# A decoder-style block on one core: the embedding projection moved ahead of its gate, the sums into X moved inside the gate tiles

## The chip, the cores and the metric

The kernel runs on 1 NeuronCore of one Trainium2 chip. The metric is device time in microseconds (us) of one launch; three runs of the kernel before gave 3404.55, 3404.18 and 3402.21, median 3404.18. PE is TensorE, DVE VectorE, ACT ScalarE, POOL GpSimd, and SP issues most of the DMAs.

## The reference

Two blocks run one after the other on a sequence of 512 tokens of width 1024, batch 1, all in float32. The first has two layers (feed-forward, attention and convolution mixer, feed-forward, and a gated per-layer embedding) and ends in a norm; the second has four layers with other mixers. The change touches only the last step of each layer of the first block:

```python
def first_block(x, p, ...):
    h = x
    for i in range(DEPTH):                       # DEPTH = 2
        h = h + 0.5 * swiglu(rmsnorm(h, g_ff1[i]), w_ff1_in[i], w_ff1_out[i])
        h = h + hybrid_mixer(rmsnorm(h, g_mix[i]), ...)
        h = h + 0.5 * swiglu(rmsnorm(h, g_ff2[i]), w_ff2_in[i], w_ff2_out[i])
        gate = sigmoid(rmsnorm(h, g_ple[i]) @ w_ple_gate[i])    # 1024 x 1024
        h = h + gate * (p[i] @ w_ple_proj[i])                   # 256 x 1024
    return rmsnorm(h, g_final)
```

The projection `p[i] @ w_ple_proj[i]` does not depend on `h`.

## The kernel before, in words

**Layout.** `X` holds h turned, as 8 chunks of 128 channels x 512 tokens. A matrix product is a `Gemm`: a list of tiles, one for each 128 output channels, each made of units of up to 8 chunks of 128 input channels. To reach float32 exactness each operand is split into a rounded high half and a low half: the activations into `UH` and `UL` (for the feed-forward's inner vector `HH` and `HL`, for the turned embedding `PH` and `PL`), the weights, loaded into `RAW` by SP, into `WH` (ACT, `high`, line 292) and `WL` (POOL, line 270). Each chunk then takes three matmuls: high x high (line 345), high weights x low activations (346), low weights x high activations (334). A unit of 8 chunks is 24 matmuls, a projection tile (2 chunks) 6. Two PSUM banks take the tiles in turn.

**Order.** Nothing is scheduled: each engine runs a list written by hand, `Step` after `Step`, and waits on semaphores in that order. Within a `Gemm`, PE runs tile n and then `tensor_tail(n)`; ACT runs `high` for a later unit, then the tile's activation (`t.act`), then `scalar_tail(n)`; DVE empties the bank of tile n and runs the tile's `vec`. In a `Gemm` with a root, ACT splits the weights of unit n + 2 between the end of tile n on PE and the activation of tile n. `high` waits for the unit two before its own.

**The norm.** The gain is in UH and UL; the factor 1/rms is applied behind the matmul, when DVE multiplies a bank by `R` (line 385, into `PRE`). A root makes R: PE sums squares over the partitions with a matmul by ones (line 490, or line 520 for one chunk of squares, 942 where the sum goes to columns), ACT takes the square root (line 495), DVE the reciprocal (line 501).

**The stage around the change**, `ple(l)`, once a layer, behind the feed-forward's output Gemm: `Gate` has 8 tiles of 8 chunks; ACT writes the sigmoid of tile c to `G[:, c, :]` (line 2200). Behind its tile 4 stand the turns of the embedding (`Flips`, 8 transposes, line 2147) and their split (lines 2152, 2155). Then `Proj`, 8 tiles of 2 chunks: DVE multiplies the bank by G (line 2210, into bank `SCALED`), adds to X (2215), and makes the next stage's low half one chunk late (`st.low`, line 911); ACT makes the high half and the square of chunk n - 1 in `scalar_tail(n)` (`st.halves`, lines 901 and 904); PE sums that square behind projection tile n (`total.tensor_chunk(n - 1)`, line 520 or 942). `Close` does chunk 7. In layer 0 the next stage is a feed-forward Gemm that reads UH and UL; in layer 1 it is the final norm, so there are no halves, and ACT also issues six loads for a later stage behind gate tile 1.

Of the kernel before, what the change touches and what calls it, by code (L numbers as in the profile page):

```python
# [117 lines left out]
def chunks(ap):  # L118
    return ap.rearrange("(c p) n -> p c n", p=P)
# [1310 lines left out]
def build(nc, out, a):  # L1430
    with ExitStack() as ctx:
# [93 lines left out]
        with ExitStack() as ph:  # L1525
            sb("GATES", [P, 2 * DC, SEQ], F32, ph)
            with ExitStack() as sub:
                sb("GAP_PLE", [P, 32], F32, sub)
                PH, PL = sb("PH", [P, 2, SEQ], F32R, sub), sb("PL", [P, 2, SEQ], F32R, sub)
                PST = sb("PST", [P, TT, PLE], F32, sub)  # L1530
# [241 lines left out]
        def ffn(l, w_in, w_out, next_gain, beside, kind=Gemm):  # L1772
# [364 lines left out]
        def ple(l):  # L2137

            nonlocal u_ready
            v = m.vec  # L2140
            wg, wp = chunks(a["w_ple_gate"][l]), chunks(a["w_ple_proj"][l])
# [19 lines left out]
            class LoadP(Step):  # L2161
                need = m.splits.total

                def issue(self, e):
                    e.wait_ge(m.splits.sem, self.need)
                    e.dma_start(PST[:], a["p"][l, 0].rearrange("(t p) f -> p t f", p=P)).then_inc(ple_in, 16)
            load_p = LoadP()
            add(load_p)
            last = l == 1
            turn_at = 4  # L2170
            u_all = m.splits.total
            fl = Flips(m, [flip_p(c) for c in range(2)], splits=2)
            fl.t0 = 0

            class Gate(Gemm):
# [8 lines left out]

                def sync_tail(self, e, i, j):
                    if j == turn_at + 1:
                        load_p.issue(e)

                def tensor_tail(self, e, i, n):
                    if n == turn_at:  # L2190
                        fl.tensor(e)

                def vector_tail(self, e, i, n):
# [3 lines left out]
                    if n == turn_at:  # L2197
                        fl.vector(e)
            add(Gate(m, 1, [Tile([(lambda i, c=c: wg[:, :, c * P:(c + 1) * P], DC, 0)], U,
                                 act=lambda e, i, pre, fun, c=c: e.activation(G[:, c, :], pre, ACT.Sigmoid))  # L2200
                            for c in range(DC)], rhs_ready=u_ready, root=Root(m, D)))
            gates = m.act_out.total
            st = Chunked(m, None if last else (lambda c: gcol("g_ff1", c + DC)))
            total = (LateColumnRoot if last else LateRoot)(m, st)

            def proj(c):
                def f(g, e, i, ps):
                    e.wait_ge(m.act_out.sem, gates)
                    e.wait_ge(*v.last)
                    e.tensor_tensor(m.SCALED, ps, G[:, c, :], ALU.mult).then_inc(*g.frees())  # L2210
                    if c > 0:
                        st.low(e, c - 1)
                    e.wait_ge(m.acc_free[g.bank(c)], g.free(0, c) + 1)
                    x = m.X[:, c, :]
                    e.tensor_tensor(x, x, m.SCALED, ALU.add).then_inc(*v.gives(m.x_new.sem, st.x0 + c + 1))
                return f

            class Proj(Gemm):


                def scalar_tail(self, e, i, n):
                    if n == 0:
                        e.activation(B.ES[:, 0:1], m.EPSC[:], ACT.Sqrt)
                    if n > 0:
                        st.halves(e, n - 1)
# [1341 lines left out]
```

## Time and profile before

| | us |
|---|---|
| median of three runs | 3404.18 |
| span of the profiled execution, first to last instruction | 3401.4 |
| PE busy | 3301.1 (97%) |
| DVE busy | 1848.6 (54%) |
| POOL busy | 1385.9 (41%) |
| ACT busy | 1113.3 (33%) |

The profiled execution has no time of its own beside its span; the median of the runs lies 2.8 us above that span. "Busy" counts the time in which an engine's instructions run, not what they wait for. PE's granted clock is near full over nearly the whole span. The stage `ple(0)` lies at about 1098 to 1168 us, `ple(1)` at about 2248 to 2317 us.

### The profile page before, as it was taken

To read this page: it belongs to the slowest core of one execution; us is meant where nothing else is said; L and a number is where in the kernel's file an instruction comes from. 1 tells how busy PE (TensorE), PEld (TensorE's weight loads), DVE (VectorE), ACT (ScalarE), POOL (GpSimd) and SP (SyncE) were. 2 spreads that over 40 slices of the span, in tenths; PEclk is the share of its full clock that TensorE was granted. 3 is DMA by queue.
4 is the path that set the end of the run, shared out by engine and by line. 5 is a ranking of instruction groups with operands and counts; after the bars stand their busy time and mean duration, and the time that the engine had idled before them with its cause. 6 is when DMAs were issued, how large, how long until landed. Compare 5 with 4: busy or idle time off the path is not lost.

```text
span 3401.4 us, 44063 instructions
## 1 busy us (share of the span) xinstructions
PE 3301.1 (97%) x16322; PEld 2611.0 (77%) x16322; DVE 1848.6 (54%) x2928; ACT 1113.3 (33%) x1836; POOL 1385.9 (41%) x691
## 2 busy tenths in 40 slices
PE   9999999999999999999999999999999999999998
PEld 7888877778888788887777888887776666777676
DVE  5532378875433464234888643335545648575753
ACT  4222234422222422223443222223234642344332
POOL 4444454444444344444544444443242223322342
PEclk9999999999999999999999999999999989999999
DMA  5333332244433334333313443344642222322221
GB/s 147 93 116 92 106 88 66 60 122 135 131 89 110 102 120 146 88 102 95 81 44 101 127 133 91 94 155 124 212 131 60 59 57 68 60 46 69 84 86 50
DMA packets 632956, 335.01 MB, mean 98 GB/s; under 512 B 97774, under 2 KB 622703, under 8 KB 631247
## 3 DMA queue, kind: packets, MB, share of 16 engines
q1 hardware_dynamic: 608062, 286.80, 30.4%
q10 hardware_dynamic: 23680, 44.32, 3.6%
q8 instruction: 110, 1.80, 0.2%
q0 software_dynamic: 1040, 1.57, 0.1%
q14 instruction: 64, 0.52, 0.0%
HBM read 308.65 MB, written 23.98 MB: 98 GB/s over the span
## 4 chain that ended last, share of the span: by engine, by line
PE 83%; DVE 11%; issue 3%; ACT 2%; POOL 0%; DVEq 0%; DMA 0%; ACTq 0%; POOLq 0%
PE ps L345 25%; PE ps L334 25%; PE ps L346 24%; PE ps L1138 2%; PE ps L1172 1%; PE ps L1162 1%; DVE UH L440 1%; PE ps L520 1%; DVE TURN L449 1%; DVE UL L443 1%; DVE ps L864 1%; DVE UL L855 0%; DVE SS L452 0%; DVE PRE L385 0%; PE ps L1289 0%
## 5 line engine op out<-in xcount | busy, mean ns | idle before, releaser
L270 POOL TENSOR_TENSOR WL<-RAW,WH 128x1024 fp32r<-128x1024 f32 (+4 forms) x606 | 1297.3, 2142 | 1977.3 <-ACT WH L292 1976.7
L345 PE MATMUL ps<-UH,WH 128*128 128x512 f32 x3056 | 1218.5, 399 | 48.1 <-DVE UL L855 16.4
L346 PE MATMUL ps<-UL,WH 128*128 128x512 f32 x3056 | 1195.8, 391 | 0.0
L292 ACT ACTIVATE WH<-RAW 128x1024 fp32r<-128x1024 f32 (+4 forms) x605 | 571.0, 945 | 1170.6 <-PE ps L334 1126.7
L334 PE MATMUL ps<-UH,WL 128*128 128x512 f32 x3056 | 802.7, 394 | 0.7 <-POOL WL L270 0.7
L345 PEld LDWEIGHTS ps<-UH,WH 128*128 128x128 f32 x3056 | 574.5, 188 | 206.5 <-issue 43.9
L334 PEld LDWEIGHTS ps<-UH,WL 128*128 128x128 f32 x3056 | 570.0, 187 | 132.9 <-issue 12.5
L346 PEld LDWEIGHTS ps<-UL,WH 128*128 128x128 f32 x3056 | 574.8, 188 | 121.4 <-issue 4.5
L345 PE MATMUL ps<-HH,WH 128*128 128x512 f32 x704 | 273.9, 389 | 0.0
L346 PE MATMUL ps<-HL,WH 128*128 128x512 f32 x704 | 273.9, 389 | 0.0
L385 DVE TENSOR_TENSOR PRE<-ps,R 128x512 f32<-128x512 f32 x144 | 99.4, 691 | 293.1 <-PE ps L334 289.4
L1782 DVE TENSOR_TENSOR ps<-ps,R 128x512 f32<-128x512 f32 x88 | 61.6, 700 | 326.7 <-PE ps L334 325.9
L458 DVE SCALAR_TENSOR_TENSOR X<-ps,X 128x512 f32 x48 | 33.1, 689 | 321.8 <-PE ps L334 321.8
L1791 ACT ACTIVATE FUN<-PRE 128x512 f32<-128x512 f32 x88 | 55.6, 632 | 425.9 <-DVE PRE L385 425.9
L334 PE MATMUL ps<-HH,WL 128*128 128x512 f32 x704 | 180.4, 389 | 0.0
L346 PEld LDWEIGHTS ps<-HL,WH 128*128 128x128 f32 x704 | 132.2, 188 | 27.4
L345 PEld LDWEIGHTS ps<-HH,WH 128*128 128x128 f32 x704 | 132.2, 188 | 27.4
L334 PEld LDWEIGHTS ps<-HH,WL 128*128 128x128 f32 x704 | 132.2, 188 | 27.4
L1879 DVE SCALAR_TENSOR_TENSOR ps<-CA,PV,ps 128x512 f32<-128x512 f32 x168 | 127.0, 756 | 6.1
L1229 ACT ACTIVATE S<-ps,NM 128x128 f32<-128x128 f32 (+3 forms) x128 | 66.3, 524 | 91.1 <-DVE NM L1186 76.8
L440 DVE TENSOR_SCALAR UH<-X,PV x48 | 91.0, 1896 | 7.7 <-DVE X L458 7.7
L1199 DVE TENSOR_SCALAR S<-S,RINV 128x128 f32<-128x128 f32 (+3 forms) x128 | 81.5, 678 | 0.0
(447 smaller groups left out, 3441.1 us busy)
## 6 DMA issues: line engine op xcount, KB each, us to landing
RAW<-w_ff_in SPq DMA_DIRECT2D x176, 512.0 KB, 3.8
RAW<-w_in SPq DMA_DIRECT2D x72, 512.0 KB, 3.9
RAW<-w_ff_out SPq DMA_DIRECT2D x64, 384.0 KB, 3.4
RAW<-w_ff_out SPq DMA_DIRECT2D x64, 320.0 KB, 3.1
RAW<-d_w_in SPq DMA_DIRECT2D x24, 512.0 KB, 3.8
CM<-cm_dram ACTq DMA_DIRECT2D x8, 1088.0 KB, 10.5
RAW<-b_w_in SPq DMA_DIRECT2D x17, 512.0 KB, 3.7
RAW<-w_out SPq DMA_DIRECT2D x16, 512.0 KB, 3.8
```

The source lines that it names most:

```text
L270: e.tensor_tensor(m.WL[:, s, 0:k, :], m.RAW[:, r, 0:k, :], m.WH[:, s, 0:k, :].bitcast(F32), ALU.subtract).then_inc(m.low_ready.sem, 1)
L292: e.activation(m.WH[:, s, 0:k, :], m.RAW[:, r, 0:k, :], ACT.Copy).then_inc(m.high_ready.sem, 1)
L334: return e.matmul(out, m.WL[:, s, c, 0:t.cols], H[:, k0 + c, :], start=False, stop=last)
L345: e.matmul(out, m.WH[:, s, c, 0:t.cols], H[:, k0 + c, :], start=(x == 0 and c == 0), stop=False)
L346: e.matmul(out, m.WH[:, s, c, 0:t.cols], L[:, k0 + c, :], start=False, stop=False)
L385: ins = t.pre(e, i, pre, ps) if t.pre else e.tensor_tensor(pre, ps, m.R[0:t.cols, :], ALU.mult)
L440: e.tensor_scalar(high, src, gain, None, ALU.mult).then_inc(*v.next())
L1138: e.matmul(out(x, n), self.q(h, n), self.k(h, n), start=True, stop=False)
L1199: e.tensor_scalar(B.S[:, r, 0:kk], B.S[:, r, 0:kk], B.RI[:, r:r + 1], None, ALU.mult).then_inc(*v.gives(m.normed.sem, self.b + a + 1))
L1229: e.activation(B.S[:, c, 0:kk], m.ps[:, 2 + x % 2, 0:kk], ACT.Exp, bias=B.NM[:, c:c + 1], accum_out=B.RS[:, c:c + 1]).then_inc(m.exped.sem, 1)
L1782: e.tensor_tensor(m.WORK, ps, m.R[:], ALU.mult).then_inc(*g.frees())
L1879: e.scalar_tensor_tensor(dst, src, wj, y, ALU.mult, ALU.add).then_inc(*v.next())
```

## The change

The embedding is loaded behind the fourth weight load of the second feed-forward, and turned and split between that feed-forward's two Gemms. `Proj` now stands before `Gate`, and ACT copies its banks to G. The product with the sigmoid and the sum into X are the `vec` of each gate tile. The square of chunk n - 1 and its sum on PE are in the tails of gate tile n. The high halves, which overwrite what the gate tiles read, are made in `Close`, behind the last gate tile. `SQ` and `ROOT` are the two halves of the buffer shown as TURN.

```diff
@@ ffn
+            g1.embed = embed
             add(g1)
...
             add(Gemm(m, (FC - HELD) // 2, pair_of_tiles(HELD // 2), vec_per_iter=4, rhs_ready=u_ready, splits=2))
+            if embed is not None:
+                embed_turns[embed] = turn_embedding(embed)
+                add(embed_turns[embed])
@@ ple (turn_embedding holds flip_p and its Flips, unchanged)
+            class Proj(Gemm):
+                def scalar_tail(self, e, i, n):
+                    b = self.bank(n)
+                    e.wait_ge(m.unit_done.sem, self.unit(i, n + 1) + 1)
+                    e.activation(G[:, n, :], m.ps[:, b, :], ACT.Copy).then_inc(m.acc_free[b], 1)
+
+                def vector(self, e):
+                    m.wait_tiles(e, self.t0 + self.nt)
+            add(Proj(m, 1, [Tile([(lambda i, c=c: wp[:, :, c * P:(c + 1) * P], 2, 0)], (PH, PL)) for c in range(DC)],
+                     rhs_ready=embed_turns[l].s0))
+
+            class Summed(Chunked):
+                def squared(self, c):
+                    return (m.SQ[:], m.T2[:], m.T[:], m.ROOT[:])[c % 4]
+
+                def square(self, e, c):
+                    e.wait_ge(m.x_new.sem, self.x0 + c + 1)
+                    if c >= 4:
+                        e.wait_ge(m.square_used.sem, self.u0 + c - 3)
+                    e.activation(self.squared(c), m.X[:, c, :], ACT.Square).then_inc(m.x_squared.sem, 1)
+
+                def high(self, e, c):
+                    e.wait_ge(m.x_new.sem, self.x0 + c + 1)
+                    e.activation(m.UH[:, c, :], m.X[:, c, :], ACT.Copy, scale=self.gain(c)).then_inc(m.x_high.sem, 1)
+
+            def gate(c):
+                def f(g, e, i, ps):
+                    e.tensor_tensor(m.SCALED, g.fun, G[:, c, :], ALU.mult).then_inc(*v.next())
+                    if last or c < DC - 1:
+                        self_add(e, c)
+                return f
+
+            def self_add(e, c):
+                x = m.X[:, c, :]
+                e.wait_ge(*v.last)
+                e.tensor_tensor(x, x, m.SCALED, ALU.add).then_inc(*v.gives(m.x_new.sem, st.x0 + c + 1))
 
             class Gate(Gemm):
                 def scalar_tail(self, e, i, n):
                     if last and n == 1:
                         e.wait_ge(m.splits.sem, u_all)
                         for k in range(SETS):
                             load_lr(e, k)
                             load_cm(e, k)
-                def sync_tail(self, e, i, j):
-                    if j == turn_at + 1:
-                        load_p.issue(e)
+                    if n > 0:
+                        st.square(e, n - 1)
 
                 def tensor_tail(self, e, i, n):
-                    if n == turn_at:
-                        fl.tensor(e)
+                    if n > 0:
+                        total.tensor_chunk(e, n - 1)
...
             class Close(Step):
                 def scalar(self, e):
-                    st.halves(e, DC - 1)
+                    e.activation(B.ES[:, 0:1], m.EPSC[:], ACT.Sqrt)
+                    if not last:
+                        e.wait_ge(m.unit_done.sem, done + 1)
+                        for c in range(2):
+                            st.high(e, c)
+                        st.square(e, DC - 1)
+                        for c in range(2, DC):
+                            st.high(e, c)
+                    else:
+                        st.square(e, DC - 1)
 
                 def vector(self, e):
-                    e.wait_ge(*v.last)
-                    st.low(e, DC - 1)
+                    if not last:
+                        st.low(e, 0)
+                        v.last = v.sem, v.n
+                        self_add(e, DC - 1)
+                        for c in range(1, DC):
+                            st.low(e, c)
                     e.wait_ge(*v.last)
@@ Opening
+            def sync_tail(self, e, i, j):
+                if self.embed is not None and j == 3:
+                    load_embedding(e, self.embed, self.u_all)
```

How the instructions stand now, first on ACT in the middle of the gate tiles of layer 0. Before, each gate tile's sigmoid (line 2200) is followed by the weight split of a later unit and the next sigmoid:

```order
L2200 ACTIVATE G<-PRE 128x512 [waits acc_free1]
L292 ACTIVATE WH<-RAW 128x1024 [waits unit_done,raw_ready2]
L2200 ACTIVATE G<-PRE 128x512 [waits acc_free0]
L292 ACTIVATE WH<-RAW 128x1024 [waits unit_done,raw_ready3]
L2200 ACTIVATE G<-PRE 128x512 [waits acc_free1]
```

In the changed kernel the sigmoid is line 2243, and the square of the chunk before is line 2203:

```order
L292 ACTIVATE WH<-RAW 128x1024 [waits unit_done,raw_ready1]
L2243 ACTIVATE FUN<-PRE 128x512 [waits acc_free1]
L2203 ACTIVATE T<-X 128x512 [waits x_new]
L292 ACTIVATE WH<-RAW 128x1024 [waits unit_done,raw_ready2]
L2243 ACTIVATE FUN<-PRE 128x512 [waits acc_free0]
L2203 ACTIVATE T<-X 128x512 [waits x_new]
L292 ACTIVATE WH<-RAW 128x1024 [waits unit_done,raw_ready3]
```

Each sigmoid is now followed by the square of the chunk before it; the weight split still stands ahead of the sigmoid.

Second, PE at the end of a gate tile of layer 0. Before, the eight low-weight matmuls of one tile are followed by the first matmul of the next:

```order
L345 MATMUL ps<-UH,WH 128x512 [waits splits]
L346 MATMUL ps<-UL,WH 128x512
L334 MATMUL ps<-UH,WL 128x512 [waits low_ready]
L334 MATMUL ps<-UH,WL 128x512 x7
L345 MATMUL ps<-UH,WH 128x512 [waits splits,high_ready,acc_free0]
L346 MATMUL ps<-UL,WH 128x512
```

In the changed kernel the sum of a square (line 520, which waits for `x_squared`) stands between them:

```order
L345 MATMUL ps<-UH,WH 128x512 [waits splits]
L346 MATMUL ps<-UL,WH 128x512
L334 MATMUL ps<-UH,WL 128x512 [waits low_ready]
L334 MATMUL ps<-UH,WL 128x512 x7
L520 MATMUL ps<-T,ONES 128x512 [waits x_squared]
L345 MATMUL ps<-UH,WH 128x512 [waits splits,high_ready,acc_free0]
L346 MATMUL ps<-UL,WH 128x512
```

The sum came here from behind the projection tiles; the next gate tile's matmuls stand behind it.

Third, ACT at the end of the gate tiles of layer 0, in the changed kernel (2254 loads the square root's table, 2207 makes a high half):

```order
L2243 ACTIVATE FUN<-PRE 128x512 [waits acc_free0]
L2203 ACTIVATE T<-X 128x512 [waits square_used,x_new]
L2254 ACT_TABLE_LOAD
L2254 ACTIVATE ESINK<-EPSC 128x1
L2207 ACTIVATE UH<-X,PV 128x512 [waits x_new,unit_done]
L2207 ACTIVATE UH<-X,PV 128x512 [waits x_new]
L2203 ACTIVATE TURN<-X 128x512 [waits square_used,x_new]
L2207 ACTIVATE UH<-X,PV 128x512 [waits x_new] x6
L292 ACTIVATE WH<-RAW 128x1024 [waits unit_done,raw_ready2]
```

Before, the high half and the square of each chunk alternate, one pair behind each projection tile. Now all eight high halves stand behind the last gate tile and the table load.

## Rows read from the trace of the kernel before

**Rows 1.** The page's chain that ended last, by engine.

```profile
PE 83%; DVE 11%; issue 3%; ACT 2%; POOL 0%; DVEq 0%; DMA 0%; ACTq 0%; POOLq 0%
```

**Rows 2.** Busy time by stretch: us, then PE, PEld, DVE, ACT, POOL, clock, DMA, GB/s.

```profile
1098.04:1180.53 82.49, 76.28 (x316) 57.58 (x314) 38.87 (x45) 34.38 (x50) 30.30 (x19) 1.00 0.29 83
2248.14:2316.57 68.43, 65.58 (x315) 52.93 (x313) 28.45 (x37) 25.44 (x38) 25.46 (x17) 1.00 0.51 171
```

**Rows 3.** Timeline of PE, first gate tiles, layer 0: start, us, engine, line, what, [idle].

```profile
1098.04 0.39 PE L345 MATMUL ps<-UH,WH 128*128 128x512 f32 x1
...
1104.01 1.13 PE L490 MATMUL ps<-SS,ONES 128*128 128x512 f32 x2 [0.37 <-DVE SS L452]
...
1105.20 0.39 PE L346 MATMUL ps<-UL,WH 128*128 128x512 f32 x1
...
1116.31 0.39 PE L345 MATMUL ps<-UH,WH 128*128 128x512 f32 x1
...
1121.75 0.39 PE L345 MATMUL ps<-UH,WH 128*128 128x512 f32 x1
```

**Rows 4.** Timeline of PE, first projection tiles of layer 0.

```profile
1144.44 0.39 PE L345 MATMUL ps<-PH,WH 128*128 128x512 f32 x1
...
1149.30 1.12 PE L520 MATMUL ps<-TURN,ONES 128*128 128x512 f32 x2 [1.28 <-ACT TURN L904]
...
1150.49 0.39 PE L346 MATMUL ps<-PL,WH 128*128 128x512 f32 x1
```

**Rows 5.** Timeline of ACT, a gate tile and the first projection tiles, layer 0.

```profile
1116.57 1.06 ACT L292 ACTIVATE WH<-RAW 128x1024 fp32r<-128x1024 f32 x1 [3.76 <-PE ps L334]
1117.54 0.61 ACT L2200 ACTIVATE G<-PRE 128x512 f32<-128x512 f32 x1
...
1146.32 1.28 ACT L2223 ACT_TABLE_LOAD   x1
1147.61 0.20 ACT L2223 ACTIVATE ESINK<-EPSC 128x1 f32<-128x1 f32 x1
...
1148.03 0.71 ACT L901 ACTIVATE UH<-X,PV 128x512 fp32r<-128x512 f32 x1
1148.64 0.61 ACT L904 ACTIVATE TURN<-X 128x512 f32<-128x512 f32 x1
```

**Rows 6.** Timeline of DVE, layer 0.

```profile
1109.98 1.35 DVE L385 TENSOR_TENSOR PRE<-ps,R 128x512 f32<-128x512 f32 x2
...
1146.22 0.70 DVE L2210 TENSOR_TENSOR ps<-ps,G 128x512 f32<-128x512 f32 x1 [0.89 <-ACT G L2200]
1146.95 0.69 DVE L2215 TENSOR_TENSOR X<-X,ps 128x512 f32<-128x512 f32 x1
...
1148.84 0.75 DVE L911 SCALAR_TENSOR_TENSOR UL<-X,PV,UH 128x512 fp32r<-128x512 f32 x1
```

**Rows 7.** Timeline of ACT and its DMA issues, layer 1.

```profile
2261.57 0.34 ACTq L2343 DMA_DIRECT2D LR<-lr_dram  x1
...
2264.30 0.42 ACTq L2348 DMA_DIRECT2D CM<-cm_dram  x1
...
2316.57 0.26 ACT L957 ACTIVATE RSUM<-ps,EPSC 128x4 f32<-128x4 f32 x1 [1.33 <-PE ps L942]
```

**Rows 8.** Waits of PE (timeline) and clock of 12 us around them (windows, PE alone).

```profile
10.14 0.47 PE L345 MATMUL ps<-UH,WH 128*128 128x512 f32 x1 [2.12 <-DVE UL L911]
...
5.00:17.00 12.00, 7.89 (x36) 1.00 1.00 296
...
2884.68 0.50 PE L345 MATMUL ps<-UH,WH 128*128 128x512 f32 x1 [2.15 <-ACT WH L292]
...
2880.00:2892.00 12.00, 9.85 (x37) 0.86 0.28 69
...
2469.05 0.47 PE L345 MATMUL ps<-UH,WH 128*128 128x512 f32 x1 [3.40 <-issue]
...
2465.00:2477.00 12.00, 8.60 (x31) 0.86 0.61 172
```

More of the change, by code:

```diff
@@ L1525, in build @@
         with ExitStack() as ph:
[L1526 to L1530, printed above, removed]
+            sb("GAP_PLE", [P, 32], F32, ph)
+            sb("HALVES_USED", [P, 2 * FC, SEQ], F32, ph)
+            PH, PL = sb("PH", [P, 2, SEQ], F32R, ph), sb("PL", [P, 2, SEQ], F32R, ph)
+            sb("TABLES_USED", [P, 832], F32, ph)
+            PST = sb("PST", [P, TT, PLE], F32, ph)
         with ExitStack() as ph:
@@ L2135, in mixer, with load_embedding, turn_embedding @@
             u_ready = g2.s0
-        def ple(l):
-            nonlocal u_ready
+        embed_turns = {}
+        def load_embedding(e, l, ready):
+            e.wait_ge(m.splits.sem, ready)
+            e.dma_start(PST[:], a["p"][l, 0].rearrange("(t p) f -> p t f", p=P)).then_inc(ple_in, 16)
+        def turn_embedding(l):
             v = m.vec
-            wg, wp = chunks(a["w_ple_gate"][l]), chunks(a["w_ple_proj"][l])
             def flip_p(c):
@@ L2173, in ple @@
             fl.t0 = 0
+            return fl
+        def ple(l):
+            nonlocal u_ready
+            v = m.vec
+            wg, wp = chunks(a["w_ple_gate"][l]), chunks(a["w_ple_proj"][l])
+            last = l == 1
+            class Proj(Gemm):
[18 more added lines that the diff above has]
+                    e.activation(m.UH[:, c, :], m.X[:, c, :], ACT.Copy, scale=self.gain(c)).then_inc(m.x_high.sem, 1)
+            u_all = m.splits.total
+            def gate(c):
[8 more added lines that the diff above has]
+                e.tensor_tensor(x, x, m.SCALED, ALU.add).then_inc(*v.gives(m.x_new.sem, st.x0 + c + 1))
@@ L2196, in vector_tail @@
                         e.memset(DEC[:, :, :, 0:1], 0.0).then_inc(*v.next())
[L2197 to L2203, printed above, removed]
@@ L2218, in ple @@
[L2218 to L2225, printed above, removed]
-                def tensor_tail(self, e, i, n):
-                    if n > 0:
-                        total.tensor_chunk(e, n - 1)
+            gates = Gate(m, 1, [Tile([(lambda i, c=c: wg[:, :, c * P:(c + 1) * P], DC, 0)], U, vec=gate(c),
+                                     act=lambda e, i, pre, fun: e.activation(fun, pre, ACT.Sigmoid))
+                                for c in range(DC)], rhs_ready=u_ready, root=Root(m, D))
@@ L2236, in vector @@
                     e.wait_ge(*v.last)
-                    st.low(e, DC - 1)
-                    e.wait_ge(*v.last)
-            add(Proj(m, 1, [Tile([(lambda i, c=c: wp[:, :, c * P:(c + 1) * P], 2, 0)], (PH, PL), vec=proj(c)) for c in range(DC)], rhs_ready=fl.s0))
             add(Close())
```

27 lines of the change are left out of this document (5 added, 22 removed).

## The prediction

> **What bounds the kernel now.** I read the chain of waits first: PE holds 83% of the chain that ended last [rows 1], so a change pays by what it takes from PE's queue or from PE's waits, and costs by each wait it puts there. Next the busy time in the two stretches that the change touches, each from the last matmul of the feed-forward's output to a fixed point: the third tile of the next feed-forward in layer 0, the square root of the norm in layer 1. They last 82.5 and 68.4 us, and PE is idle for 6.2 and 2.9 of them [rows 2]. That is all that a better order could win: 9.1 us. Then the timelines of PE, ACT and DVE, for what one gate tile and one projection tile cost and who hands over to whom. A gate tile is 24 matmuls, and its period is 1121.75 - 1116.31 = 5.44 us, 0.227 a matmul, without idle time [rows 3]; DVE, ACT and POOL finish their part of it beneath PE.
>
> **The change, part by part.**
>
> *What leaves.* The entry of Gate: PE waited 0.37 us for the sum of squares [rows 3]; with 10.9 us of projection in front this wait is gone. The waits of PE behind projection tiles, such as 1.28 us [rows 4], go too. The late product, sum and halves between them cost nothing extra any more; what is late next is worked out below.
>
> *Projection in front.* 8 tiles x 6 matmuls x 0.227 = 10.9 us of PE. ACT has a split of 256 columns and a copy per tile, together below a tile's 1.36 us (an ACT pass over 512 columns is 0.61 [rows 5], a 256-column split less); I count no wait inside. At the end stands the 1.06 us split of the first gate unit [rows 5]. It comes behind the copy of tile 6: 0.25 us for the wake-up, 0.5 for the copy, 1.06 for the split, together 1.8 after tile 6 ends, against 1.36 for tile 7, and POOL's low half follows later still. Bound below: 0, if everything hides; above: 2.5 us, a split and an ACT pass in full and a wake-up. I take 1.1.
>
> *Turn of the embedding.* 8 transposes, about 0.9 us of PE, taken from behind gate tile 4 and put between two Gemms of the feed-forward: 0.9 out of my stretches and 0.9 in elsewhere. Its four DVE passes (about 3 us) lie beneath a feed-forward tile of 22 chunks, 66 x 0.227 = 15 us. Its load moves on SP's queue from behind the sixth gate load to behind the fourth feed-forward load. It waits there for the previous stage's splits, and the fifth load waits behind it; SP is four units, over 20 us, ahead of PE, so nothing. Without that cover it would cost the few us that a load takes.
>
> *The square's sum in the gate tiles.* This decides. PE's queue now holds, between gate tiles n and n + 1, the sum of the square of chunk n - 1. The square is ready only when ACT has made it, and on ACT it stands behind the sigmoid of tile n, which needs the bank that PE has only just finished; and ahead of the sigmoid stands the split of unit n + 2. X of chunk n - 1 itself has long been there. Let S be the moment at which PE would start the next tile, 1116.31. The split starts at S + 0.26, the sigmoid at S + 1.23 and ends at S + 1.84 [rows 5]; ACT starts its next pass 0.1 before the end of the last (1148.03 + 0.71 against 1148.64), so the square ends at S + 2.36. PE follows within 0.05 (1148.64 + 0.61 against 1149.30 [rows 4, 5]): 2.41 us of waiting. All gate tiles behind it in PE's queue wait too, and with them everything else. The sum itself, from 1149.30 to the second matmul behind it at 1150.49, less 0.23, is 0.96 us; it merely moved here. Five tiles a layer (n = 2 to 6) wait 2.41: 12.1 us.
>
> *Tile 1* is worse. R is late: PE's sum of squares is at 1104.01, DVE's first product with R at 1109.98 [rows 3, 6], ending about 1110.7. The line S lies at 1105.20 - 0.23 + 5.44 = 1110.41. Behind that product now stand, one after the other: sigmoid 0 (to 1111.3), product with G 0.70 and sum into X 0.69 with a wake-up (to 1113.0), the product with R for tile 1 (to 1113.7), sigmoid 1 (to 1114.4), square 0 (to 1114.9): PE goes on at S + 4.5. In layer 1 the six loads that ACT issues from 2261.57 to 2264.72 [rows 7] stand between sigmoid 1 and square 0. They begin when the sigmoid is let go, 3.4 after S, last 3.15, then the square 0.61: S + 7.3.
>
> *End of layer 0.* With S now the end of gate tile 7. There is no split ahead: before, the product behind the last sigmoid starts at 1146.22, that is 1144.44 + 1.8 [rows 4, 6], so that sigmoid ends about S + 1.6. Square 6 ends at S + 2.1, its sum on PE at S + 3.1. Then ACT: table load 1.28 and the dummy root 0.2 to S + 3.6, high half 0 to S + 4.2 [rows 5]; DVE low half 0, 0.75 [rows 6], to S + 5.1. Only now can PE start the feed-forward. The sum into X of chunk 7 delays square 7 to about S + 6.3, then six high halves at 0.63 end at S + 10.1, the last low half at S + 10.9. The first tile ends at S + 11.6, then the sum 0.96 and the second tile 5.44: S + 18.0. The Trainium skill ("ScalarE: Activation LUTs", What ACT_TABLE_LOAD costs) puts a drain of about 1.38 us beside the load's 1.28. In the profile the dummy root starts at 1147.61, right behind 1146.32 + 1.28 [rows 5], so no drain stands behind it; with one, each layer would be 1.4 us longer.
>
> *End of layer 1.* The same to S + 3.6, then square 7 to S + 4.1 and the square root of the sum about 1.3 later (2316.57 less PE's wait, sum and hand-over, cf. [rows 7]): S + 5.4.
>
> **The sum**, in us:
>
> | | layer 0 | layer 1 |
> |---|---|---|
> | projection and hand-over | 10.9 + 1.1 | 10.9 + 1.1 |
> | 8 gate tiles | 43.5 | 43.5 |
> | root sum, six sums of squares | 1.0 + 5.8 | 1.0 + 5.8 |
> | wait at tile 1 | 4.5 | 7.3 |
> | waits at tiles 2 to 6 | 12.1 | 12.1 |
> | behind tile 7 | 18.0 | 5.4 |
> | turn, elsewhere | 0.9 | 0.9 |
> | total | 97.8 | 88.0 |
> | before | 82.5 | 68.4 |
>
> That is + 15.3 and + 19.6, together + 34.9 us.
>
> **The clock.** Waits can cost a second time. Of two waits of PE near 2.1 us, one left the granted clock at 1.00 over its 12 us, one left 0.86; a wait of 3.40 left 0.86 too [rows 8]. A mean of 0.86 over 12 us is 3.4 us at half (1.2 instead of 2.4 GHz), in which PE does 1.7 us less work. The change makes ten waits of 2.4 us and two long ones. If half the ten cost 1.7 and the two long ones about 2 each (the clock may fall inside the wait and must still come back behind it), that is 8.5 + 4 = 12.5. Bounds: 0 (no fall) and about 22 (each one falls: 10 x 1.7 + 2 x 2.5). I take the middle, as the rows nearest in length split evenly.
>
> So 34.9 + 12.5 = 47.4 on a span of 3401.4: 3448.8. The median of the runs lies 2.8 above that span; the forecast is 3404.2 + 47.4 = 3451.6, say 3451.
>
> **Rivals.**
>
> *The waits come, the clock holds* (12%): 3404.2 + 34.9 = 3439. For it: after the 2.12 us wait it did hold. Against it: a 2.15 us wait lowered it.
>
> *Every wait drops the clock* (10%): 34.9 + 22 = 57, 3461. For it: the 2.15 us wait did, and here the waits come in a series, one every 8.8 us. Against it: the 2.12 us wait. The Trainium skill ("TensorE: Matmul & The Clock Gate", HAM oscillation — how this bites in real kernels) describes just this, a kernel whose every tile ends in a wait and which falls back to the slow clock tile after tile; no row of this kernel has such a series. If the clock did not come back between waits at all, twelve tiles of 5.44 us would run at half and the time would near 3404.2 + 34.9 + 65 = 3504 (3% more).
>
> *The squares are in time* (4%), the case on the other side. If the square of chunk n - 1 were made before PE ends tile n, the 12.1 of both layers and most of tile 1's 4.5 and 7.3 would vanish: about 36 us, which leaves the total 1 us below before: 3403. It decides at one point: ready before S or not. X of the chunk is ready 3 us before S; but ACT's order, in which the square stands behind the sigmoid of the tile just finished, speaks against it. A half-way version, in which hand-overs overlap more than I think and each wait is 1 us, is part of this (3%): about 3415.
>
> *The forecast* (71%): 3442 to 3460.
>
> **How the numbers follow.** What a measurement can tell from no change is about 0.2%, 6.8 us. Slower by more than that are the forecast, both clock rivals and the half-way version: 0.95. The squares in time would be the same rather than faster, since 1 us is below 0.2%: same 0.04, faster 0.01. The likeliest case has 3451. The range takes in the low end of "clock holds" and the high end of "every wait": 3434 to 3464; it leaves out the squares in time and a clock that never recovers.
>
> **What would show it.** The sum of a square (line 520, in layer 1 line 942) behind gate tiles 2 to 6 should have an idle time of about 2.3 us before it, released by ACT, line 2203 (the trace counts idle from the modelled end of the last matmul, about 0.15 later than S). Behind tile 1 4.4 in layer 0 and 7.2 in layer 1. A gate tile's period should be 8.8 us at full clock. PE should wait about 2 us for the first low half of the feed-forward in layer 0, and the projection tiles should follow each other at 1.36. The span from the last output matmul to the third feed-forward tile should be near 97 plus what the clock costs. Wrong would be: idle times of PE behind gate tiles below 1 us; the projection in front paced by ACT or POOL at clearly more than 1.36; or a longer stretch somewhere else, as where the turn now stands.

## The result and the profile after

Slower. Four runs of the changed kernel gave 3466.47 to 3470.40 us, median 3468.81; four of the kernel before gave a median of 3403.61. The ratio is 1.0189, 95% interval [1.0177, 1.0201]. The forecast was 3451, the range ended at 3464: the sign and, as will be seen, the waits were right, the time lies 4.8 us outside.

The profiled execution, the fastest of the four, has a span of 3464.7, 63.3 more than before. PE still holds the same share of the chain that ended last [rows 1]:

```profile
PE 83%; DVE 10%; issue 3%; ACT 2%; POOL 0%; DVEq 0%; ACTq 0%; POOLq 0%
```

The two stages, from the first projection matmul to the points of [rows 2] (columns: us, PE busy, clock, DMA share, GB/s):

```profile
1100.45:1210.25 109.80, 89.49 (x307) 0.88 0.25 71
2280.41:2381.04 100.63, 78.89 (x307) 0.84 0.39 129
```

They last 109.80 and 100.63 us against 82.49 and 68.43, so 27.3 + 32.2 = 59.5 of the 63.3 us lie here. Read the third number too: the mean granted clock is 0.88 and 0.84, where [rows 2] show 1.00. PE at the gate tiles of layer 0, to hold against [rows 3]:

```profile
1100.45 0.39 PE L345 MATMUL ps<-PH,WH 128*128 128x512 f32 x1
...
1112.23 0.47 PE L345 MATMUL ps<-UH,WH 128*128 128x512 f32 x1 [0.30 <-issue]
...
1128.97 1.15 PE L520 MATMUL ps<-TURN,ONES 128*128 128x512 f32 x2 [4.04 <-ACT TURN L2203]
...
1139.42 1.35 PE L520 MATMUL ps<-T,ONES 128*128 128x512 f32 x2 [2.25 <-ACT T L2203]
...
1149.87 1.56 PE L520 MATMUL ps<-T,ONES 128*128 128x512 f32 x2 [2.25 <-ACT T L2203]
...
1191.43 1.12 PE L520 MATMUL ps<-T,ONES 128*128 128x512 f32 x2 [1.97 <-ACT T L2203]
1194.55 0.54 PE L345 MATMUL ps<-UH,WH 128*128 128x512 f32 x1 [1.99 <-DVE UL L911]
```

And in layer 1, where [rows 7] had the loads:

```profile
2311.77 1.86 PE L942 MATMUL ps<-ONES,TURN 128*128 128x1 f32 x8 [6.88 <-ACT TURN L2203]
...
2323.45 1.05 PE L942 MATMUL ps<-ONES,T 128*128 128x1 f32 x8 [2.25 <-ACT T L2203]
```

Each sum of a square (L520, L942) waits for ACT's L2203. The waits are 4.04 and 6.88 us behind tile 1, 2.25 behind tiles 2 to 6, 1.97 behind tile 7. The first gate matmul stands at 1112.23, and 1128.97 to 1139.42 is one gate tile with its sum and its wait: 10.45 us, where the matmuls, the sum and the wait alone would give 5.44 + 0.96 + 2.41 = 8.81 (8.84 in the filled kernel below). ACT in such a tile, to hold against [rows 5]:

```profile
1137.27 1.06 ACT L292 ACTIVATE WH<-RAW 128x1024 fp32r<-128x1024 f32 x1 [8.35 <-PE ps L334]
1138.23 0.61 ACT L2243 ACTIVATE FUN<-PRE 128x512 f32<-128x512 f32 x1
1138.76 0.61 ACT L2203 ACTIVATE T<-X 128x512 f32<-128x512 f32 x1
```

The order is the one that was read from the code: split, sigmoid, square, and nothing of it begins before PE ends the tile (the sum follows at 1139.42). What the period has over 8.84 is in the clock, PE alone, one row a microsecond:

```profile
1139.00:1140.00 1.00, 0.58 (x3) 1.00 0.00 0
1140.00:1141.00 1.00, 1.00 (x3) 0.59 0.00 0
1141.00:1142.00 1.00, 1.00 (x4) 0.50 0.08 24
1142.00:1143.00 1.00, 1.00 (x4) 0.50 0.98 289
1143.00:1144.00 1.00, 1.00 (x4) 0.70 0.70 212
1144.00:1145.00 1.00, 1.00 (x6) 1.00 0.00 0
```

Behind the wait PE runs at half for over three microseconds and then at full again, until the next wait. It does so behind all ten waits of 2.25 us; behind one of them, at tile 5 of layer 1, it runs at half for 6.8 us and not 3.4.

### The profile page after: what moved, and what is told of

Read it like the earlier page. It is cut to its first block, busy times and chain, and to the rows that moved or that the text cites. A ratio compares the mean times of both kernels' runs of the same rounds, so it can differ in the third digit from the quotient of the medians.

```text
span 3464.7 us, 44068 instructions
## 1 busy us (share of the span) xinstructions
PE 3333.0 (96%) x16322; PEld 2629.3 (76%) x16322; DVE 1864.5 (54%) x2928; ACT 1120.3 (32%) x1852; POOL 1386.2 (40%) x691
## 3 DMA queue, kind: packets, MB, share of 16 engines
q0 software_dynamic: 1040, 1.57, 0.1%
## 4 chain that ended last, share of the span: by engine, by line
PE 83%; DVE 10%; issue 3%; ACT 2%; POOL 0%; DVEq 0%; ACTq 0%; POOLq 0%
PE ps L345 25%; PE ps L334 24%; PE ps L346 24%; PE ps L1138 2%; PE ps L1172 1%; PE ps L1162 1%; PE ps L520 1%; DVE UH L440 1%; DVE TURN L449 1%; DVE ps L864 1%; ACT WH L292 1%; DVE SS L452 0%; DVE UL L855 0%; DVE PRE L385 0%; POOL WL L270 0%
## 5 line engine op out<-in xcount | busy, mean ns | idle before, releaser
L345 PE MATMUL ps<-UH,WH 128*128 128x512 f32 x3056 | 1236.1, 404 | 49.6 <-DVE UL L855 15.9
L345 PEld LDWEIGHTS ps<-UH,WH 128*128 128x128 f32 x3056 | 582.1, 190 | 214.5 <-issue 50.6
L346 PEld LDWEIGHTS ps<-UL,WH 128*128 128x128 f32 x3056 | 582.1, 190 | 126.0 <-issue 7.5
```

What stands on the lines that cost most here:

```text
L345: e.matmul(out, m.WH[:, s, c, 0:t.cols], H[:, k0 + c, :], start=(x == 0 and c == 0), stop=False)
L346: e.matmul(out, m.WH[:, s, c, 0:t.cols], L[:, k0 + c, :], start=False, stop=False)
```

## The experiments

Each kernel is built from the changed one, and its times stand beside runs of the kernel before on the same chip (medians 3402.5 to 3404.7). "Stage 0" and "stage 1" are the two stretches above.

### The squares one tile earlier

```diff
@@ Gate.scalar_tail
-                    if n > 0:
-                        st.square(e, n - 1)
+                    if n < DC - 1:
+                        st.square(e, n)
```

> ACT makes the square of chunk n (not n - 1) behind the sigmoid of tile n, for tiles 0 to 6; PE's sum stays where it is, one tile later. Nothing is left out. Theory (the waits for the square and the clock falls behind them are the whole loss): each square is ready about 3 us after its tile ends, well before PE ends the next one, so the waits of 2.25 us on line 520 and 942 go, the clock stays at full through the gate tiles, the long waits at tile 1 go or shrink to below 1 us, and the gate tile's period is 5.44 + 0.96 = 6.4 us; the stages fall from 109.8 and 100.6 us to about 82 and 69, the time to about 3402, that is back to the kernel before within 0.2%. Rival (the projection placed in front and the turn placed between the feed-forward's Gemms cost something of their own, by their queues or loads): the time stays above 3412 although the waits are gone.

Measured: 3423.55 median (3414.56 to 3427.41, five runs), ratio 1.006 [1.0047, 1.0074]. PE in layer 0:

```profile
1127.46 1.12 PE L520 MATMUL ps<-TURN,ONES 128*128 128x512 f32 x2 [2.92 <-ACT TURN L2203]
...
1133.88 1.02 PE L520 MATMUL ps<-T,ONES 128*128 128x512 f32 x2
...
1140.22 1.02 PE L520 MATMUL ps<-T,ONES 128*128 128x512 f32 x2
...
1170.33 0.70 PE L345 MATMUL ps<-UH,WH 128*128 128x512 f32 x1 [3.70 <-DVE UL L911]
```

The waits of 2.25 us are gone and a tile with its sum takes 6.34 to 6.42 us, so the theory of the waits holds. The stages fell to 85.94 and 73.07, not to 82 and 69: of the time lost, 45 us came back and 21 by the median did not (11 in the profile, which is of the fastest run). The wait at tile 1 shrank only to 2.92, where below 1 was expected: R comes late, the square of chunk 0 has two DVE passes and a sigmoid ahead of it, and this wait is not one of ACT's order. Behind the last tile PE waits 3.70 for the first low half. Between the two stages and ahead of them the time is within 2 us of before apart from the turn, so the rival that the projection in front costs much of its own falls. Its number, above 3412, came true all the same, and the theory's 3402 did not: the waits at tile 1 and behind the last tile, which the theory had below 1 us or left out, stayed.

For the spread of its runs it was run again:

> The kernel with early squares once more, for a second profile: its five runs spread from 3414.6 to 3427.4 at a mean clock of 0.987 to 0.984, and the profile on record is of the fastest. Theory: the same waits end in another pattern of clock falls (the 2.92 us wait at tile 1 of layer 0 held the clock in the one profile, and dropped it in the kernel with the plain close), so where the time is longer, the busy time of PE is longer at half clock in places where the waits are the same. Rival: a wait is longer in the slower runs.

3423.8 median of two. The waits are the same to 0.01 us (2.92 and 3.70 in layer 0, 2.92 in layer 1), but at tile 1 of layer 0 the clock fell (it had held the first time), and in layer 1 it stood at half for 6.8 us behind tile 1 instead of 3.4 (clock in rows of one microsecond). So the same wait costs 0, 1.7 or 3.4 us more. The spans of the two profiles are 3412.8 and 3421.9, 9.1 apart, and 3.5 of it lie in the two stages. Over the whole span PE is busy 3309.2 and 3315.9 us with the same 16322 matmuls, so 6.7 of the 9.1 are matmuls that ran slower, and 2.4 are more idle time, outside the waits named. The theory holds for the larger part, between these two executions; the rival for the rest.

### The close without the early table load

```diff
@@ Close.scalar, beside the edit of the experiment before
-                    e.activation(B.ES[:, 0:1], m.EPSC[:], ACT.Sqrt)
                     if not last:
-                        for c in range(2):
+                        for c in range(DC):
                             st.high(e, c)
                         st.square(e, DC - 1)
-                        for c in range(2, DC):
-                            st.high(e, c)
                     else:
+                        e.activation(B.ES[:, 0:1], m.EPSC[:], ACT.Sqrt)
                         st.square(e, DC - 1)
```

> The early squares of the first experiment, and in layer 0, behind the last gate tile, no table load and dummy root ahead of the high halves: ACT makes the eight high halves at once, then the square of chunk 7; the table is loaded when the root wants it. Nothing is left out. Theory: the feed-forward's first low half starts 1.28 + 0.2 us earlier, since high half 0 stood behind the load; PE's wait of 2 us there shrinks to about 0.6, and if the clock fell behind it that goes too; 2 to 4 us faster than the first experiment, about 3399, at or just below the kernel before. Rival: the low halves on DVE set the first feed-forward tile's pace anyway, or the table load lands in the root's path ahead of the second tile and costs its 1.28 us there: same as the first experiment within 1 us.

3414.61 median (3412.97 to 3416.97), ratio 1.0036 [1.0022, 1.0050], where about 3399 was expected. PE's wait for the first low half fell from 3.70 to 2.18 us: the 1.5 expected, but not down to 0.6, since it had stood at 3.70 and not at 2. Stage 0 is 84.90 against 85.94: here the clock fell at tile 1 (3.4 us at half), and behind the last tile it stood at half for 3.4 us instead of 6.8. The medians differ by 9 us. The waits show 1.5 of it; the spans of the profiles, 3413.3 and 3412.8, do not show the rest, as the first kernel was profiled in its fastest run.

### The sums two tiles behind

```diff
@@ Gate.tensor_tail, beside both edits above
-                    if n > 0:
-                        total.tensor_chunk(e, n - 1)
+                    for c in (n - 2,) if 1 < n < DC - 1 else (n - 2, n - 1) if n == DC - 1 else ():
+                        total.tensor_chunk(e, c)
```

> The early squares and plain close of the earlier experiment, and PE sums the square of chunk n - 2 behind gate tile n (chunks 5 and 6 behind tile 7). Nothing is left out. What is left of the loss in the kernel with early squares is put down to three places: PE's wait of 2.92 us at tile 1 in both layers with its fall of the clock (1.7 more where it falls), the wait behind tile 7, and the turn, 0.9. Theory: the wait at tile 1 goes in both layers, 2 x 2.92 and one or two falls of 1.7 with it, so 7.5 to 9 us less than 3414.6: 3406, the same as the kernel before within 0.2%. Rival (the rest of the loss is noise of the chip or lies elsewhere in the kernel): it stays within 3 us of 3414.

3404.37 median of eleven runs (3400.61 to 3406.73) against 3404.68 of fifteen: ratio 0.9998 [0.9989, 1.0007]; 3406 was expected. The whole loss is gone. PE's idle times above 0.4 us in the stages are these:

```profile
1164.16 0.47 PE L345 MATMUL ps<-UH,WH 128*128 128x512 f32 x1 [1.33 <-DVE UL L911]
...
1165.33 0.50 PE L345 MATMUL ps<-UH,WH 128*128 128x512 f32 x1 [0.46 <-DVE UL L911]
...
2312.86 1.86 PE L942 MATMUL ps<-ONES,TURN 128*128 128x1 f32 x8 [1.88 <-ACT TURN L2203]
```

Stage 0 lasts 79.57 (1099.02 to 1178.59), 2.9 less than before, stage 1 67.79 (2246.97 to 2314.76), 0.6 less; the two turns, about 1 each, and 2.2 us behind stage 1 take that back. Behind stage 1 the two kernels are the same; PE is busy there 0.95 us longer with the same 5798 matmuls (1020.06 against 1019.11) and idle 1.26 longer, and why is open. In stage 0 the clock fell once, for 3.4 us, behind the two waits of 1.33 and 0.46. With its lists in this order the change costs nothing and gives nothing.

### Work in the place of the wait

```diff
@@ Gate.tensor_tail
                     if n > 0:
+                        for _ in range(10 if n < DC - 1 else 0):
+                            e.matmul(m.ps[:, 2, :], m.UH[:, 1, 0:P], m.UH[:, 0, :], start=True, stop=True)
                         total.tensor_chunk(e, n - 1)
```

> Ten matmuls of 128 x 512, whose result nobody uses, stand in PE's queue ahead of the sum of the square behind gate tiles 1 to 6; they take 10 x 0.227 = 2.27 us, as long as PE waits there in the changed kernel. They are work added for the experiment. Theory (the loss is waiting time plus a fall of the clock behind each wait): the period of a gate tile stays at the 8.84 us that it has at full clock with the wait, and the clock no longer falls between tiles 2 and 7, so the period is 8.8 instead of 10.45 and the time falls by 10 x 1.6 = 16 us plus one or two at tile 1 (3450 to 3454). Rival (the tile's period of 10.45 has another cause than the clock, such as a slower hand-over or matmuls that wait for the weights' halves): the added matmuls add to it or leave it, and the time stays at 3468 or rises.

3446.27 median (3445.58 to 3451.49), 22.5 less than the changed kernel, by adding work. PE:

```profile
1136.47 1.13 PE L520 MATMUL ps<-T,ONES 128*128 128x512 f32 x2
...
1145.31 1.13 PE L520 MATMUL ps<-T,ONES 128*128 128x512 f32 x2
```

The period is 8.84 us: the wait is still paid, the fall is not, and between tiles 2 and 7 the clock's rows are at 1.00 in both layers. So the rival, a period with another cause than the clock, is out. It gave more than the 16 expected (20.9 by the spans), as the fall behind tile 1 of layer 0 went too (1.77 us of wait are left of 4.04), and so did the one of double length in layer 1.

With five in place of ten:

> Five such matmuls (1.13 us) in place of ten, so that 1.1 us of each 2.25 us wait is left. They are work added for the experiment. Theory A (the clock falls only behind idle time of about 2 us and more): the clock holds between tiles 2 and 7, as with ten, and the time is the same, 3450 to 3454. Theory B (any wait in this series drops it, or it follows the busy share): it falls as in the changed kernel or by part of it, period 9.5 to 10.4 us, time 3460 to 3468. At tile 1 some 3 to 5 us of wait are left in either, and the clock falls there.

3457.06 median (3456.48 to 3457.24). Both theories were right in one layer each:

```profile
1147.97 1.12 PE L520 MATMUL ps<-T,ONES 128*128 128x512 f32 x2 [1.11 <-ACT T L2203]
...
1156.82 1.12 PE L520 MATMUL ps<-TURN,ONES 128*128 128x512 f32 x2 [1.11 <-ACT TURN L2203]
...
1147.97:1156.82 8.85, 7.74 (x32) 1.00 0.21 59
...
2322.75 1.05 PE L942 MATMUL ps<-ONES,T 128*128 128x1 f32 x8 [1.11 <-ACT T L2203]
...
2333.22 1.05 PE L942 MATMUL ps<-ONES,TURN 128*128 128x1 f32 x8 [1.11 <-ACT TURN L2203]
...
2322.75:2333.22 10.47, 9.36 (x38) 0.84 0.18 52
```

The wait is 1.11 us in both. In layer 0 the period is 8.85 and the clock 1.00, in layer 1 10.47 and 0.84, behind all five waits. What is seen to differ is the sum behind the wait: in layer 0 two matmuls of 512 columns (1.12 us), in layer 1 eight of one column (L942, 1.05 us).

With three in layer 0 and seven in layer 1:

> Three filling matmuls a gate tile in layer 0 (a wait of 2.25 - 0.68 = 1.57 us is left) and seven in layer 1 (0.66 us left, and behind it the sum of 1.05 us, whose eight matmuls have one column each). Added work. With five, layer 0 kept 1.11 us of wait and held the clock, while layer 1 kept 1.11 too and lost it behind every tile. Theory A (the one-column sum is as good as idle for the clock, so layer 1 stood idle for 2.16 us): with 0.66 + 1.05 = 1.71 us layer 1 holds or falls as layer 0 does with 1.57; if both hold, periods are 8.85 in both layers and the time is near the filled kernel's 3446. Theory B (layer 1 falls for another reason, such as the longer wait at tile 1 ahead of it, 5.63 us): layer 1 falls again, period 10.45, 3455.

3451.56 median (3448.85 to 3452.37). The clock held behind all five waits in both layers (1.57 us in layer 0; 0.66 in layer 1, period 2324.47 - 2315.58 = 8.89), though the wait at tile 1 of layer 1 was 5.20 us and dropped it. That is what theory A said. In layer 1, a wait of 1.11 us with 1.05 us of one-column matmuls behind it fell five times in five, a wait of 0.66 with the same never. But the run changed the wait and not the kind of sum, so that the one-column sum makes the difference between the layers is argued and not shown: no run has the same sum in both. The median is 5 us above the 3446 of the theory, of which the profiles show 3.3 in the stages (101.96 and 91.50 against 99.81 and 90.36): the wait at tile 1 of layer 0, 3.36 us here, dropped the clock.

### Split behind the square

```diff
@@ Gemm.scalar, for the gate tiles from 1 on
-                if ahead and j + 2 <= self.nu and self.u0 + j + 2 < len(m.unit_k):
+                more = ahead and j + 2 <= self.nu and self.u0 + j + 2 < len(m.unit_k)
+                late = self.split_late and n > 0
+                if more and not late:
                     self.high(e, i, j + 2)
...
                 self.scalar_tail(e, i, n)
+                if more and late:
+                    self.high(e, i, j + 2)
```

> In the gate tiles from 1 on ACT runs sigmoid, square and then the weight split, instead of split, sigmoid, square. Nothing is left out. The wait of PE is then the bank's product with R on DVE, the sigmoid and the square: 1.97 us of idle time, as behind tile 7, where no split stands ahead, instead of 2.25. Theory (waits set the stage; each fall costs 1.65): ten waits lose 0.28 each, 3 us, and if at 1.97 us the clock still falls that is all, 3465 to 3466; if at 1.97 it holds, another 16 us go and the time is near 3449. The rival is that the later split makes PE wait for weights, the next period grows by it, and the time rises.

3462.6 median (3459.16 to 3465.79), 6 less than the changed kernel, where 3 were expected. The waits are 1.96 or 1.97 us, and the clock fell behind each of the ten; the periods are 10.14 to 10.25. So the cover for the split was there (PE never waited for weights), and 1.97 us is enough for a fall. The spans of the two profiles differ by 2.6, as expected; what the medians have beyond that stays open.

### The loads behind the square

```diff
@@ Gate.scalar_tail
+                    if n > 0:
+                        st.square(e, n - 1)
                     if last and n == 1:
                         e.wait_ge(m.splits.sem, u_all)
                         for k in range(SETS):
                             load_lr(e, k)
                             load_cm(e, k)
-                    if n > 0:
-                        st.square(e, n - 1)
```

> In layer 1 the six loads that ACT issues behind the sigmoid of tile 1 stand behind the square of chunk 0 instead of ahead of it. Nothing else differs. Prediction's account (the wait of 6.88 us at tile 1 of layer 1 is the late R, 4.0 as in layer 0, plus the loads' 3): it falls to about 4.0 us, layer 0 does not change, and the loads, 3.15 us long, end before ACT's next split is wanted or push it by below 1 us: 3 to 4 us faster than the changed kernel, 3465. Rival (the loads only move the delay to the next split and sigmoid, tile 2's wait grows by as much): same as the changed kernel within 1 us.

PE's wait at tile 1 of layer 1 fell from 6.88 to 4.08 us:

```profile
2307.47 1.87 PE L942 MATMUL ps<-ONES,TURN 128*128 128x1 f32 x8 [4.08 <-ACT TURN L2203]
```

Tile 2's wait stayed at 2.25, stage 1 is 97.74 instead of 100.63, 2.9 less. The median, 3467.34 (3465.29 to 3468.92), is 1.5 less, which four runs cannot tell from nothing. The spans are only 0.4 apart, as the stretch behind stage 1, where the kernels are the same, is 4.0 longer here (1087.6 against 1083.7). The profile shows the step, the time does not.

### Half as many waits

```diff
@@ Gate.tensor_tail
-                    if n > 0:
-                        total.tensor_chunk(e, n - 1)
+                    for c in {2: (0, 1), 4: (2, 3), 6: (4, 5), 7: (6,)}.get(n, ()):
+                        total.tensor_chunk(e, c)
```

> PE sums the squares behind gate tiles 2, 4 and 6 only (two chunks each) and behind tile 7 (one), so there are half as many waits, about 16 us apart instead of 8.8. The same sums are made. In layer 0 the waits at tiles 2, 4, 6 keep their 2.25 us since the later of the two squares is made behind the sigmoid of the tile just finished; tile 1's wait moves to tile 2 and is partly covered. Theory 1 (each wait of 2.25 us drops the clock by itself, whatever its neighbours): three falls a layer of about 1.65 us each remain, and the time falls by some 2 x (2 x 3.9 + 3 to 5) = 20 to 26 us to 3442 to 3448. Theory 2 (the clock falls because the waits come in a series 8.8 us apart): with 16 us between them it holds, and the time falls by some 8 us more, to 3434 to 3440. In the clock's rows: 0.5 behind each of the waits, or full.

3428.28 median (3426.30 to 3429.89), lower than either theory. The expectation of the wait failed: the first sum of a pair fills 1 us of it, so PE waits 1.39 us, not 2.25:

```profile
1136.12 1.02 PE L520 MATMUL ps<-TURN,ONES 128*128 128x512 f32 x2
1138.53 1.12 PE L520 MATMUL ps<-T,ONES 128*128 128x512 f32 x2 [1.39 <-ACT T L2203]
```

In layer 0 the clock held at all three. In layer 1, whose pair is one-column matmuls with 0.9 to 1.5 us of wait between them, it fell at two of three. The run says nothing on waits of 2.25 us far apart, so others were made for it.

### The same wait, alone and in a series

Ten filling matmuls behind tiles 1, 2, 4 and 5 leave a wait of 2.25 us at tiles 3 and 6, 26 us apart:

```diff
+                        for _ in range(10 if n in (1, 2, 4, 5) else 0):
```

> As the kernel filled with ten matmuls a gate tile, but tiles 3 and 6 are left unfilled: each layer keeps two single waits of 2.25 us, 26 us apart, each behind two or three tiles at full clock, beside the waits at tiles 1 and 7. The filling matmuls are added work. Theory 1 (each such wait drops the clock by itself): the clock's rows show a fall of 3.3 us at half behind all four, and the time is 4 x 1.65 = 6.6 us above the filled kernel, 3453. Theory 2 (the series is needed, or it is chance): none to two of the four fall, 3446 to 3450.

3456.24 median (3453.95 to 3457.00), 10 above the filled kernel and above both theories. The profiles are 11.4 apart: 6.2 in the stages (101.77 and 94.60 against 99.81 and 90.36) and 5.2 outside, where the kernels are the same. The clock in the 5 us behind each of the four waits:

```profile
1148.00:1153.00 5.00, 4.53 (x18) 1.00 0.36 104
1175.00:1180.00 5.00, 5.00 (x13) 0.66 0.38 107
2326.00:2331.00 5.00, 5.00 (x27) 1.00 0.35 105
2353.00:2358.00 5.00, 5.00 (x15) 0.50 0.36 105
```

Two of four fell. The same kernel again:

> The kernel with two single waits a layer (tiles 3 and 6) once more: in its first profile the waits at tile 3 held the clock at 1.00 in both layers and those at tile 6 dropped it. If where the wait stands in the program decides, the same two fall again; if it is chance, another two or another number.

3455.17 median of two. The same two fell (0.72 and 0.50 over the 5 us) and the same two held. That speaks against a coin tossed anew at every wait, though four coins would repeat so once in sixteen times; what in the program's course decides was not found.

Filled behind tiles 1, 3 and 5, so that the waits are 17.7 us apart:

```diff
+                        for _ in range(10 if n in (1, 3, 5) else 0):
```

> Ten filling matmuls (added work) behind tiles 1, 3 and 5, so tiles 2, 4 and 6 wait 2.25 us, 17.7 us apart (19.3 with a fall). Theory S (waits need to be close for every one to fall): two to four of the six fall, as of the single waits 26 us apart. Theory T (the distance does not matter, any wait that follows a fall falls too): once one has fallen, all later ones of the layer fall.

3452.07 median of two. Four of six fell: in layer 0 tiles 2 and 4 and not 6, in layer 1 tiles 2 and 6 and not 4. Theory T is out.

No wait ahead of tile 3 in layer 0, then four of 2.25 us, 8.8 apart:

```diff
+                        for _ in range(22 if n == 1 else 10 if n == 2 else 0):
```

> Filling matmuls (added work) only behind tiles 1 (22, 5 us) and 2 (10), so in layer 0 there is no wait of PE ahead of tile 3, and tiles 3 to 6 wait 2.25 us each, 8.8 us apart at full clock. Theory S (the series does it): the first wait may hold or fall like a single one, but from the second on every one falls, at least three falls in each layer, period 10.45 between the falls. Theory C (each wait is a draw of about one in two, and the changed kernel's twelve of twelve were luck or came from the long wait at tile 1 ahead): four to five falls of the eight waits, with periods of 8.85 and 10.45 mixed.

The clock in the 5 us behind the four waits of layer 0, then of layer 1:

```profile
1148.00:1153.00 5.00, 5.00 (x22) 1.00 0.38 108
1156.00:1161.00 5.00, 4.58 (x11) 0.66 0.35 101
1167.00:1172.00 5.00, 5.00 (x14) 0.69 0.36 105
1177.00:1182.00 5.00, 4.73 (x19) 1.00 0.36 106
2324.00:2329.00 5.00, 5.00 (x16) 0.50 0.36 105
2336.00:2341.00 5.00, 5.00 (x19) 0.66 0.38 105
2346.00:2351.00 5.00, 4.61 (x18) 0.67 0.37 104
2357.00:2362.00 5.00, 5.00 (x20) 0.66 0.37 108
```

3460.76 median of two. Six of eight fell. Theory S wanted a fall at every wait from the second on, and the fourth of layer 0 held: refuted as it stood. Theory C wanted four or five; eight draws of one half give six or more about once in seven times, so this run does not rule it out. The layers differ in one more thing: in layer 1 a wait of 1.89 us at tile 1 had dropped the clock before the series, and all four fell; in layer 0 nothing had, and two of four fell. Whether a fall ahead keeps such a series falling was not tested.

## Why the prediction was wrong

**The waits: right.** Counted from S (0.15 before the trace's idle time starts), the waits were 2.40, 4.2 and 7.0 us against 2.41, 4.5 and 7.3; the wait for the first low half 1.99 against 2; the projection with its hand-over 17.97 - (5.97 - 0.37) = 12.4 us (from the first projection matmul to the root's sum, less the same stretch of before without its wait [rows 3]) against 10.9 + 1.1; the turn 1.04 against 0.9. In both stages together PE is idle 42.1 us, 33.0 more than before. The filled kernel shows the sum: 3446 with some 6 us of clock left in it, where the rival without falls had 3439. The early squares show the cause: one line on ACT, and 45 us come back.

**The clock: wrong, and this is the step that failed.** "If half the ten cost 1.7 and the two long ones about 2 each" gave 12.5. Measured: stage 0 109.8 against 96.9 forecast without clock, stage 1 100.6 against 87.1 (88.0 less the turn): 12.9 + 13.5 = 26.4. By the periods, 10.45 - 8.84 = 1.61 for each of the ten: 16.1, all of them and not half. The rest is what the sum priced too low or left out: the long waits at tile 1, 1.6 and about 2.9 (in layer 1 the clock stood at half for 6.0 us behind the wait); one fall of twice the length in layer 1, 1.6; and behind tile 7, where the waits of 1.97 and 1.99 us make a fall of their own, the remaining 4.2, which the sum had at nothing. The price of one fall, 1.7, was right. The stretches at half, PE alone: behind tile 1 and the double one in layer 1, then behind tile 7 in both layers:

```profile
2311.77:2317.78 6.01, 6.01 (x18) 0.50 1.03 413
2355.33:2362.15 6.82, 6.82 (x20) 0.50 0.27 77
...
1194.79:1201.62 6.83, 6.38 (x15) 0.50 0.00 0
2379.22:2381.04 1.82, 1.78 (x8) 0.50 0.00 0
```

At half clock half of the busy time is the price: for the last two rows 4.1 us, which is what the sum had at nothing.

**The rival that came true** is "every wait drops the clock". I gave it 10% and 3461, and its own bound, 22, was 4 short by the falls behind tile 7. The Trainium skill ("TensorE: Matmul & The Clock Gate", HAM oscillation — how this bites in real kernels) describes it, for a kernel whose tiles end in a wait for DMA; this trace agrees for waits on ACT, with ten falls in ten. I weighed two single waits of before [rows 8], one that held and one that fell, as if the series were draws of one half. For single waits the half was near: 26 us apart two of four fell, the same two in both profiles, and 17.7 us apart four of six. At 8.8 us six of eight fell in the series of four. In the unbroken series every one fell: ten here, and ten each in the kernels with the loads and with the split moved. Those with filled matmuls have less idle time as well as fewer waits, and the unbroken series stand behind a long wait at tile 1 that dropped the clock, so the distance is a possible reason, not a shown one. Which single wait drops the clock stays open. The prediction also said that no row of before has such a series. It has one of shorter waits, behind the projection tiles: 1.28 [rows 4], 1.58, 1.35 and 1.07 us, some 6 us apart, and the clock stood at 1.00 over the whole stage [rows 2].

**Table load.** ACT behind tile 7 of layer 0 in the changed kernel, timeline:

```profile
1190.77 0.61 ACT L2203 ACTIVATE T<-X 128x512 f32<-128x512 f32 x1
1191.40 1.28 ACT L2254 ACT_TABLE_LOAD   x1
1192.69 0.20 ACT L2254 ACTIVATE ESINK<-EPSC 128x1 f32<-128x1 f32 x1
1192.80 1.32 ACT L2207 ACTIVATE UH<-X,PV 128x512 fp32r<-128x512 f32 x2
```

The dummy root follows the load within 0.01 us, as in [rows 5]: no drain stands behind it. The square behind the last sigmoid ends 0.02 us before the load starts, so none stands ahead of it either.

**Outside the stages** 63.3 - 59.5 = 3.8 us were added: two turns, 2, and 1.8 more. PE is busy there 5.4 us longer, 2.1 of them the turns and 3.3 the same matmuls run slower, and idle 1.6 less. As two profiles of one kernel differ outside the stages by more than that (5.6 us in the early squares), the change need not be the cause.

## What to carry to other kernels

Before a matmul is put behind a tile on PE, read on the other engine's list whether its operand is made before or after that tile's own activation: one line too late made every tile wait 2.4 us. Then price each wait of about 2 us twice, once as time and once as 1.6 us of clock, and in an unbroken series of them take the full price for every one. If the operand cannot come earlier, sum it a tile or two later, or give PE other work in between.

## What the runs showed of the hardware

Matmuls that nobody needs, put into the waits, made the changed kernel 22.5 us faster, and the clock's rows between tiles 2 and 7 went from falls to 1.00. Waits of 2.25 and 1.97 us in an unbroken series dropped the clock ten times in ten each; five waits of 1.57 us and five of 1.11 beside sums of 512 columns never did. A wait of 1.11 us with 1.05 us of one-column matmuls behind it, which the profile counts as busy, dropped it five times in five. And one and the same wait of 2.92 us, in two profiles of one kernel, once held the clock and once dropped it; of the 9.1 us between these two spans 6.7 were matmuls that ran slower.
